# Moving every stage-local tile 192 bytes up in SBUF, and reordering the DMA issues of the opening

## What is computed

```python
c_act = jax.nn.silu(c)
mod = c_act @ w_ada[l] + b_ada[l]
h = _rmsnorm(x, norm_attn_g[l]) * (1.0 + sc1) + sh1
proj = h @ w_in[l]
```

## Time and profile before

| | us |
|---|---|
| median of 3 runs | 3691.44 |
| lowest, highest | 3690.61, 3695.4 |
| the profiled execution, its own time | 3694.67 |
| its span, first to last instruction | 3692.6 |
| TensorE busy in the span | 3500.5 (95%) |
| VectorE busy | 2148.6 (58%) |
| ScalarE busy | 1032.2 (28%) |
| GpSimd busy | 131.7 (4%) |
| mean granted TensorE clock | 0.956 |

### The profile page before, as it was taken

The page is one execution under the profiler, slowest core; times in us unless marked ns, Lnnn a source line. Parts: engine busy times, 40 slices in busy tenths (PEclk is TensorE's granted clock), DMA queues, the critical chain, the costliest instruction groups (busy, mean ns, idle before and its releaser), DMA issues. The chain is left out here.

```text
span 3692.6 us, 49234 instructions
## 1 busy us (share of the span) xinstructions
PE 3500.5 (95%) x19911; PEld 2848.3 (77%) x19911; DVE 2148.6 (58%) x4936; ACT 1032.2 (28%) x1604; POOL 131.7 (4%) x116
## 2 busy tenths in 40 slices
PE   5988899999999999899999999989999999999998
PEld 3655867887888888774688888878888886578886
DVE  6554656567667575754455757576656636543334
ACT  3354023223321212242432121222121125432222
POOL 0012010000000000100000000010000010000000
PEclk7998879999999999898999999989999999999998
DMA  8532024444334343320123434333343313023331
GB/s 170 139 98 68 3 69 126 120 126 112 86 87 115 97 114 93 105 79 13 29 61 94 110 97 113 90 106 86 103 108 98 104 51 109 12 75 97 95 94 63
DMA packets 646939, 333.95 MB, mean 90 GB/s; under 512 B 31659, under 2 KB 642935, under 8 KB 646456
## 3 DMA queue, kind: packets, MB, share of 16 engines
q1 hardware_dynamic: 646388, 330.68, 33.0%
q10 hardware_dynamic: 324, 0.13, 0.0%
HBM read 328.61 MB, written 2.77 MB: 90 GB/s over the span
## 5 line engine op out<-in xcount | busy, mean ns | idle before, releaser
L2099 PE MATMUL psum<-hn_high,high 128*128 128x512 f32 (+1 forms) x3136 | 1128.7, 360 | 8.5 <-DVE low L2544 8.5
L2100 PE MATMUL psum<-hn_low,high 128*128 128x512 f32 (+1 forms) x3136 | 1119.2, 357 | 0.0
L2101 PE MATMUL psum<-hn_high,low 128*128 128x512 f32 (+1 forms) x3136 | 1119.1, 357 | 0.0
L2629 DVE SCALAR_TENSOR_TENSOR partial<-stage,cond,partial 128x128 f32<-128x128 f32 x2592 | 701.9, 346 | 1.0 <-DMA stage<-in_w_ada 0.9
L2099 PEld LDWEIGHTS psum<-hn_high,high 128*128 128x128 f32 x3136 | 593.4, 189 | 124.5 <-issue 20.4
L2101 PEld LDWEIGHTS psum<-hn_high,low 128*128 128x128 f32 x3136 | 593.0, 189 | 91.8
L2100 PEld LDWEIGHTS psum<-hn_low,high 128*128 128x128 f32 x3136 | 593.0, 189 | 89.5 <-issue 0.5
L2544 DVE TENSOR_TENSOR low<-stage,high 128x1024 fp32r<-128x1024 f32 (+2 forms) x415 | 493.0, 1208 | 187.3 <-ACT high L1778 186.9
L1778 ACT ACTIVATE high<-stage 128x1024 fp32r<-128x1024 f32 (+2 forms) x415 | 415.2, 1025 | 512.8 <-DMA stage<-in_w_ffn 361.7
L2099 PE MATMUL psum<-hidden_high,high 128*128 128x512 f32 (+1 forms) x1408 | 501.9, 356 | 1.8 <-DVE hidden_low L2549 1.8
L2100 PE MATMUL psum<-hidden_low,high 128*128 128x512 f32 (+1 forms) x1408 | 500.0, 355 | 0.0
(11 more groups left out here) (316 smaller groups left out, 2966.9 us busy)
## 6 DMA issues: line engine op xcount, KB each, us to landing
stage<-in_w_ffn SPq DMA_DIRECT2D x240, 512.0 KB, 4.2
stage<-in_w_ada SPq DMA_DIRECT2D x768, 128.0 KB, 2.8
stage<-in_w_in SPq DMA_DIRECT2D x48, 512.0 KB, 4.7
stage<-in_w_out SPq DMA_DIRECT2D x24, 512.0 KB, 4.0
stage<-in_w_ffn SPq DMA_DIRECT2D x32, 384.0 KB, 3.7
stage<-in_w_gate SPq DMA_DIRECT2D x22, 512.0 KB, 3.9
stage<-in_w_up SPq DMA_DIRECT2D x22, 512.0 KB, 5.1
stage<-in_w_down SPq DMA_DIRECT2D x16, 512.0 KB, 4.0
```

The costliest lines, as they stand in the source:

```text
L2099: self.e.matmul(out, high[:, i], xh, start=first and n == 0, stop=False)
L2100: self.e.matmul(out, high[:, i], xl, start=False, stop=False)
L2101: done = self.e.matmul(out, low[:, i], xh, start=False, stop=last and n == nk - 1)
L2629: self.e.scalar_tensor_tensor(acc, view[:, k, :], by, acc, ALU.mult, ALU.add).then_inc(*inc)
```

## The change

It adds two alignments of the allocator. The stage-local tiles begin at the next address that is 192 modulo 512 (103616 in place of 103424), and the first block's `delta_base` at the next that is 64 modulo 128 (150976 in place of 150688, so 288 bytes further up). Moving operands now begin at 192 modulo 512 in the feed-forwards, the mixers and the first block's `mixed`, and at 448 in the first block's `hn`. `stage`, `high`, `low`, `tmp` and all other permanent tiles stay where they are.

In the opening all three conditions (twelve DMAs) are issued on ScalarE's queue, ahead of everything else there. The second and third count on a semaphore of their own, and `load_start` on SyncE has no wait for the sigmoid any more. The first four `w_ada` blocks go ahead of the identity and the five rows on SyncE's queue. (The line that adds `load_conditions` to the list of empty default methods is left out.)

```diff
--- before.py
+++ after.py
@@ -44,6 +44,7 @@
 TURNED = 32
 MISC = 24
 QROWS = D // 32
+ROW, LANE = 512, 192
 COMPUTE = ("tensor_wrote", "scalar_wrote", "vector_wrote", "pool_wrote")
 
 
@@ -181,6 +182,7 @@
         self.mean_main, self.mean_ctx = sb("mean_main", [P, SEQ]), sb("mean_ctx", [P, CTX])
         self.token_gates = sb("token_gates", [P, P])
         self.small_consts = sb("small_consts", [P, P])
+        self.at += (LANE - self.at) % ROW
         self.phase_base = self.at
         self.ps = ctx.enter_context(nc.psum_tensor("psum", [P, 8, 512], F32))
         self.rows_by_head = nc.dram_tensor("rows_by_head", (HEADS1, SKEW), F32, kind="Internal").ap()
@@ -258,6 +260,7 @@
         self.DX = self.tiled("delta_qkv", 12, SEQ + 3)
         self.DD = self.DX[:, :, 0:SEQ]
         self.G, self.EG, self.BT = (self.area("gate_rows", SEQ)[0:8] for _ in range(3))
+        self.at += (LANE - self.at) % 128
         delta_base = self.at
         self.hn_first = self.halves("hn", KT, SEQ)
         self.QA, self.KA, self.VA = (self.tiled("qkv", 4, SEQ) for _ in range(3))
@@ -732,9 +735,10 @@
     def setup(self):
         mem = self.mem
         self.clear()
-        self.load_first()
+        self.load_conditions()
         if self.board.plan is not None:
             self.load_to(STAGES - 1)
+        self.load_first()
         self.take_condition(0)
         self.take_vectors(0, 1)
         self.load_start()
...
@@ -1616,25 +1620,14 @@
 
 
     def load_first(self):
-        self.load_condition(0, self.mem.inp["c"][0])
         self.dma(self.misc(), ("eye",), self.mem.eye[:], self.mem.const["eye"])
         self.wait_ge("cleared")
         for n, (tile, dst, src) in enumerate(self.mem.rows):
             if tile == 0:
                 self.dma(self.misc(), ("row", n), dst, src)
 
-    def load_condition(self, n, c):
-        rows = c.rearrange("(p r) -> p r", r=QROWS)
-        for q in range(4):
-            self.dma_counts["cond_landed"] = self.dma_counts.get("cond_landed", 0) + 16
-            self.e.dma_start(self.mem.cond_rows[32 * q:32 * q + 32, n, :], rows).then_inc(self.sems["cond_landed"], 16)
-        self.board.new["cond_rows", n] = "cond_landed", self.dma_counts["cond_landed"]
-
     def load_start(self):
         mem, i = self.mem, self.mem.inp
-        self.wait_ge("cond_sigmoid", 0)
-        self.load_condition(1, i["c_2"][0])
-        self.load_condition(2, i["c_ctx_2"])
         col = lambda ap: ap.rearrange("(n o) -> n o", o=1)
         self.dma(self.misc(), ("tokens", "main"), mem.tokens_main, i["x"][0].rearrange("(a p) n -> p a n", p=P))
         self.dma(self.misc(), ("small", 0), mem.dt_bias, col(i["dt_bias"][0]))
@@ -1814,10 +1807,17 @@
         self.wait_each(part.hn_free)
         self.e.activation(high, xs, ACT.Identity, bias=shift).then_inc(*self.mark("norm_high", name, k))
 
+    def load_conditions(self):
+        i = self.mem.inp
+        for n, c in enumerate((i["c"][0], i["c_2"][0], i["c_ctx_2"])):
+            sem, rows = "cond_landed" if n == 0 else "conds_landed", c.rearrange("(p r) -> p r", r=QROWS)
+            for q in range(4):
+                self.dma_counts[sem] = self.dma_counts.get(sem, 0) + 16
+                self.e.dma_start(self.mem.cond_rows[32 * q:32 * q + 32, n, :], rows).then_inc(self.sems[sem], 16)
+            self.board.new["cond_rows", n] = sem, self.dma_counts[sem]
+
     def condition(self, n, x, t):
-        self.wait_ge("cond_rows", n)
-        if n == 1:
-            self.wait_ge("cond_rows", 2)
+        self.wait_ge("cond_rows", 2 if n else 0)
         self.wait_free(t)
         self.e.activation(t.ap[:, 0:QROWS], x, ACT.Sigmoid).then_inc(*self.mark("cond_sigmoid", n))
 
@@ -3008,7 +3008,7 @@
     board = Board()
     with ExitStack() as ctx:
         mem = Memory(nc, ctx, inp, const, out)
-        landed = [f"{n}_landed" for n in ("out", "skew", "rows", "cond", *(f"stage{i}" for i in range(STAGES)),
+        landed = [f"{n}_landed" for n in ("out", "skew", "rows", "cond", "conds", *(f"stage{i}" for i in range(STAGES)),
                                          *(f"misc{i}" for i in range(MISC)))]
         sems = {n: ctx.enter_context(nc.semaphore(n)) for n in (*COMPUTE, *landed)}
         for name, program in ENGINES.items():
```

More of the change, by code:

```diff
@@ L1603 @@
     modulation_vector = clear = load_start = turn_vectors = condition = turn_tokens = distance_tables = idle
-    load_first = distance_rows = store_distances = skew_distances = token_square = token_pair = token_pair_sums = turn_context = gate_logs = gate_sums = gate_exps = turn_gates = load_bias = attention_scores = attention_turn = attention_values = idle
+    load_first = load_conditions = distance_rows = store_distances = skew_distances = token_square = token_pair = token_pair_sums = turn_context = gate_logs = gate_sums = gate_exps = turn_gates = load_bias = attention_scores = attention_turn = attention_values = idle
     attention_normalise = head_square = head_roots = head_spread = gains = clear_pads = gate_row = idle
```

## The result

| | before | after |
|---|---|---|
| median, us | 3691.72 (4 runs) | 3634.59 (4 runs, 3630.63 to 3642.83) |
| ratio, 95% interval | | 0.9846 [0.9828, 0.9865] |
| the profiled execution, its own time | 3694.67 | 3635.35 |
| mean granted TensorE clock | 0.956 | 0.965 |

The kernel is 57 us faster. The direction was right and the size was not.

What follows compares the result with a forecast made beforehand. TensorE was taken as the bound, after a short opening in which it waits. Opening 5.5, first block 0.8 and 256-column rhythm 3.6 made 9.9 us, so 3681.5 us against the median of 3691.44; range 3642 to 3695.

Steps and rivals of the forecast that it cites:

- the rows a little later: Opening, SyncE's queue: fourth `w_ada` block at 13.6 us, rows a little later, so VectorE starts its sums at 13.9.
- The tokens need 8.5 us from issue to use: Opening: tokens issued at about 11.05 us are used at 19.6, and the fifth block follows 3.4 us behind, at 23.0.
- 5.5 us with bounds 3.1 to 5.9: Opening: VectorE starts the fifth block at 23.05 in place of 28.60 us, 5.5 us earlier; bounds 3.1 and 5.9.
- the small gain on the 256-column rhythms: 256-column matmuls: a new address may hold the shorter of two rhythms, 3.6 us gained; likeliest case as summed, chance 0.34.
- the first block's 0.8 us: First block's `w_in` and `w_out`: tiles no longer 32 bytes off, 0.9 ns on 864 matmuls, 0.8 us gained.
- The load's conflict goes: Rival, split matmuls: new offset keeps weights' load and moving stream apart, 3.2 ns each gives 3642 us; chance 0.24.
- the 40-column loads: Stretch where 18 of 39 loads bring 40 columns, not 128: 232.3 against 233.3 ns, giving 3.2 ns for 128 columns.
- Its other price: Conflict rival's far end: all 6.2 ns a matmul costs besides its columns saved on each, giving 3601 us.
- Addresses do nothing: Rival, split matmuls: only the opening and the first block's 0.8 us count, 3685.1 us; chance 0.24.
- Collides more: Rival, all 13,536 split matmuls: load meets the moving tile longer, 1.8 ns each gives 3710 us; chance 0.10.
- The opening gives nothing: Rival, opening: moved rows hold VectorE, or tokens and fifth block crowd each other, 5.5 us lost again, 3691; chance 0.08.
- a shifted start could move where the clock falls: Sign of error: the whole moves by more than the opening while start-to-start distances stay; no size given.

Runs made afterwards that it cites:

- rows_first: The kernel after, with the identity and the five rows issued ahead of the first `w_ada` blocks again: 3636.17 us.
- open_only: The kernel after without the two alignments, so only the opening's new order against the kernel before: 3685.81 us, ratio 0.9982.
- low_moved: The kernel before with only the `low` weight buffers 64 bytes further up: 3686.92 us beside 3693.41.
- addr_only: The kernel before with only the two alignments added, the opening as before: 3637.93 us beside 3691.13.
- lane128: The kernel after with `LANE` at 128 in place of 192, so moving tiles at distance 0 from the weights: 3637.18 us.
- lane64: The kernel after with `LANE` at 64 in place of 192, so moving tiles at distance 192 from the weights: 3679.59 us.

## Why the prediction was wrong

**The opening: right mechanism, sizes off.** Two steps had the wrong size. The first is "the rows a little later" than the fourth block: TensorE used `conv_w` 5.2 us behind its issue, and VectorE started 2.4 us later than I took. The second is "The tokens need 8.5 us from issue to use": in rows_first, where TensorE does wait for them, it is 11.1 us, and the fifth block is there at 24.73 and not at 23.0. In the kernel after, VectorE came to it at 25.15, so its own lateness hid this second error. Where I had 5.5 us with bounds 3.1 to 5.9, the fifth block gave 3.45, the first matmul on `hn` 4.7, and open_only 5.3 by the medians.

**The addresses: this is the step that failed.** I had written that the small gain on the 256-column rhythms, half of 1.5 ns on 4,824 matmuls, was the weakest term, taken "by the row nearest in kind". With the first block's 0.8 us the sum had 0.8 + 3.6 us, where the traces have 53. Two rhythms at one address showed how much timing alone shifts the pace at that distance; they were no measure of another distance. Nor did the 512-column matmuls outside the first block get a term at all, and they gave over half of the gain.

**The rival "The load's conflict goes" had nearly the right price, in part by luck.** Its 3.2 ns came from the 40-column loads, and the runs gave 3.4 to 3.5 ns at 512 columns and 3.6 at 256. But those rows tell what a smaller load saves at the old address, and no run ties that to what another distance saves. At distance 0 the saving is 5.4 ns at 512 columns and none at 256. Nor is the conflict gone at distance 64, where 512 columns still take 2.3 ns more than at distance 0 (229.0 against 226.7). What the runs show is that the distance between weights and moving tile sets the pace; that the weights' load is what meets the moving stream stays argued, since low_moved did not settle it. I gave the case 0.24, since no row showed the conflict absent. But none could have: the tiles of the kernel before stood at distance 128 or, in the first block, at 32, and distance 32 ran at 233.3 ns. Its price, "3691.4 - 43 - 6 = 3642", fell 7 us short. I counted 13,536 matmuls from the earlier trace rows, where the trace has 14,976 with `mixed` and the other forms; each gave 0.2 to 0.4 ns more than 3.2; and about 3 us came with fewer matmuls at 1.2 GHz. The opening gave 1 us less than the 6 in that price.

**The range** began at 3642, which is that rival's price itself and leaves nothing for an error of the price on the fast side. That is why even the rival that came nearest missed. Its other price, 6.2 ns on each matmul and 3601 us, was left out, though the single best rhythms are 5.9 ns below the kernel before at 512 columns (226.7) and 5.8 at 256 (113.3); no kernel here had both.

**The other rivals.** "Addresses do nothing" is refuted by addr_only. By the Trainium skill, "SBUF — State Buffer", section "Who interferes with whom", TensorE waits on nobody and reads weights and moving operand through independent ports. TensorE's pace here changes by 6.6 ns with the distance between the two (lane128 against lane64, where one number of the allocator differs), and it changes too when the weight buffers alone move (weights_moved), so for this stream the measurement decides against it; no run shows where in the chip the two meet. "Collides more" exists, but at distance 192 and at 32 and 224, and with 0.7 ns in place of 1.8: lane64 shows it at 512 columns, and gains at 256. "The opening gives nothing" is refuted by open_only.

**The clock.** I had said that a shifted start could move where the clock falls, and that I'd be wrong if the whole moved while the distances stayed. They did not stay. The time at 1.2 GHz is 65 us shorter after the change, 41 of it in the opening, where TensorE waits much of the time (it is 280 us in open_only, which gains only 5). On the split matmuls the clock gave about 3 us.

## What to carry to other kernels

Where TensorE loads new 128x128 weights under every matmul, the byte distance between weight and moving tiles, modulo 256, is a parameter to sweep: one number in the allocator was worth 1.4% here, between distance 64 or 0 and distance 128. Sweep it for each column count by itself, since the best distance differs. And when a price rests on one indirect row, put an error of that price on both sides into the range, and don't end the range at the price itself.

## What was new about the hardware

- Start to start of a float32-rounded matmul that loads 128x128 weights, at 2.4 GHz: 226.7, 229.0, 232.4 and 233.3 ns with 512 columns at distances 0, 64, 128 and 192; 120.0, 113.3 or 117.8, 118.5 to 120.1, and 117.1 ns (the mean) with 256. At distances 32 and 224, which only the first block's tiles had, 512 columns took 233.2 to 233.3 ns. The two lowest are 544 and 272 cycles, 17 for each 16 columns, and nothing here ran faster. The Trainium skill, "TensorE: Matmul & The Clock Gate", section "Back-to-back issue gap", has 512/2.4 + 2.5 = 215.8 ns as the gap of an isolated matmul; the lowest rhythm here, 226.7 ns, is 10.9 above it.
- A stream can fall into a rhythm and keep it: at one distance and one shape 113.3 or 117.8 ns, 229.0 or 233.3 ns, for up to 1,572 matmuls. rows_first and the kernel after differ in their opening alone, and have 116.6 and 115.5 ns at 256 columns. I read the kernel's spread from run to run, 12 us, as such rhythms, but only one execution of each kernel has a trace, so this is not shown.
- A small row that is issued behind 2 MB on the same queue is used by TensorE 5.2 us behind its issue and by the copy that follows 5.6 us behind it. In the kernel before that copy came 2.6 us behind the issue, and in rows_first TensorE used the row 2.2 us behind it.
